# A decoder step with 32 routed experts on one core: slots of a tile numbered across groups of four partitions, and another order of work in the last three tiles

## The chip, the cores and the metric

The kernel runs on one core of a Trainium2 chip. The metric is the device time of one launch in microseconds (us), the median of several runs. A clock of 1 of TensorE (PE) is full speed; the profile calls VectorE DVE, ScalarE ACT, GpSimd POOL and the synchronisation engine SP. SP and POOL issue most of the transfers, and sixteen DMA engines carry them out.

## What is computed

One layer for 576 tokens (512 of a prompt and 64 of a sample) of 1024 channels, all in float32:

```python
m, new_pool, new_conv = _mixer(x, ...)            # w_in, pooling and short convolution, w_out
x = _layer_norm(DEEPNORM_ALPHA * x + m, ln1_g, ln1_b)
f = _hier_moe(x, ...)                             # top-1 of 4 groups, then top-2 of its 8 experts
x = _layer_norm(DEEPNORM_ALPHA * x + f, ln2_g, ln2_b)
...
for e in range(N_EXPERTS):                        # 32 experts, d_expert 512
    hdn = jax.nn.silu(xf @ w1[e]) * (xf @ w3[e])
    acc = acc + combine[:, e:e + 1] * (hdn @ w2[e])
```

Each token goes to two experts, so there are 1152 assignments. Every expert has three matrices of 2 MB (w1, w3, w2), 201 MB in all. By the reference's routing of the given inputs the experts get between 15 and 74 tokens, 36 on average.

## The kernel before, in words

**Front part** (to about 230 us). The mixer, the first layer norm, the router and a small index computation on DVE. DVE counts tokens and gives every assignment a tile and a slot in it.

**Tiles.** A tile is up to 64 tokens of one expert. There are 33 tiles, numbered 0 to 32 (E is 32): one per expert, and a second one for the expert with 74. `hot_first` and `hot_col` are one-hot comparisons of an assignment's slot number with a row of 64 numbers, `iota`, which holds 0 to 63. So slot s of a tile stands at position s of 64, the tokens of an expert fill positions 0, 1, 2 and so on, and the rest of the 64 are empty. From these tables come `token_row`, `pair_row`, `first_row`, `final_row` and `sample_row`, the lists of row numbers for GpSimd's indirect transfers. An empty position has a row number out of range, and nothing is moved for it.

**A tile on PE** (`tile(t)`, `into_hidden` L701, `turn_hidden` L714, `down` L722): w1 product (L710, 32 matmuls into bank B1), w3 product (L710, 32 matmuls), transposition of the hidden rows (L719), w2 product (L731, 16 matmuls of 512 columns). Two tiles share one fetch of x and one transposition of it (`turn_pair`, L698). Up to tile 30 (`STAGGERED`) the w2 product of tile t-1 is done within tile t. From tile 30 on each tile does its own too, so the program of PE ends: w1(30), w3(30), w2(29), w2(30), w1(31), w3(31), w2(31), w1(32), w3(32), w2(32). Positions 0 to 63 of SBUF hold channels 0 to 511 of the result of a tile, and 64 to 127 hold channels 512 to 1023 of the same 64 tokens.

**The other engines.** ACT: `silu_of(t)` (L950) after the w1 product, `spread(t)` (L992, a square root) for the second layer norm, `keep_xeT`, `fill` (the residual). DVE: `products(t)` (L1493) multiplies silu, gate and w3 product and frees PE to transpose; `keep_hT(t)` (L1498) copies the transposed hidden rows, for which w2(t) waits; `add_y(t)` (L1504) takes the result out of PSUM; `final(t)` (L1510 to L1529, 13 instructions) is the second layer norm of the tokens whose second expert is tile t. In `final`, L1528 waits for ACT's `spread(t)`.

**GpSimd's transfers** (2 KB per token and half, 4 KB per token for the fetch): `fetch` (L1107) gathers x for two tiles, `store(t)` (L1085) scatters the results of tokens for which t is the first of their two experts into `first_outputs`, `load(t)` (L1089) gathers those of the tokens for which t is the second, `send(t)` (L1093, L1097) scatters finished rows to the two outputs. `load(t)` waits for `store(t-1)` to have landed.

**Weights.** SP issues the loads of the 99 matrices in the order of use (`LOADS`) into ten blocks of 2 MB in SBUF; a block is loaded again once PE has used it. Each of these loads lies over all 128 partitions and is spread over the 16 DMA engines. PE waits for a block until all 16 have finished their part. The last w2 is loaded in two halves with a semaphore each (`last_half`).

Of the kernel before, what the change touches and what calls it, by code (L numbers as in the profile page):

```python
# [7 lines left out]
BF16 = mybir.dt.bfloat16  # L8
I32 = mybir.dt.int32
ALU = mybir.AluOpType  # L10
# [3 lines left out]
P = 128  # L14
D = 1024
KD = D // P
# [87 lines left out]
def build(nc, x_prompt, x_sample, state_pool, state_conv, w_in, w_pool_map, pool_scale, conv_w, w_out,  # L104
# [3 lines left out]
    with ctx:  # L108
        def sem(name):
            return ctx.enter_context(nc.semaphore(name))  # L110
# [66 lines left out]
        ones = sb("ones", [P, P], BF16)  # L177
        iota = sb("iota", [P, SLOTS])
        rev = sb("rev", [P, EPG])
        edges = sb("edges", [P, NQ])  # L180
        tokval = sb("tokval", [P, NT])
        row_shift = sb("row_shift", [P, 1])
        half_of = sb("half_of", [P, 1])
        chan = sb("chan", [P, NG, 4])
# [150 lines left out]
        more_first = sem("more_first")  # L335
        last_loaded = sem("last_loaded")
        prev_cleared = sem("prev_cleared")
        prev_loaded = [sem(f"prev_loaded{w}") for w in range(ZR)]
# [27 lines left out]
        def _(sp):  # L366
# [64 lines left out]
            def load(n):  # L431
                kind, t = LOADS[n]
                if kind == "w2" and t == E:
# [63 lines left out]
        def _(pe):  # L497
# [202 lines left out]

            def into_hidden(kind, b, loads, seq, i):  # L701

                done, bank = (h1_done, B1) if kind == "w1" else (h_done, B3)
                w = in_block(b)
                wait(pe, silu_ready if kind == "w1" else h_ready, seq)
                pe.wait_ge(block_loaded[b], loads)
                for k in range(KD):
                    x = xeT[:, k, i * SLOTS:(i + 1) * SLOTS]
                    for g in range(2):
                        mm = pe.matmul(ps[64 * g:64 * g + 64, bank, 0:FH], x, w[:, k, g * FH:(g + 1) * FH],  # L710
                                       start=(k == 0), stop=(k == KD - 1))
                mm.then_inc(done, 1)
# [38 lines left out]
            def tile(t):  # L751

                if t % 2 == 0:
                    pe.wait_ge(xeT_ready, t + 2)
                into_hidden("w1", *place("w1", t), t, t % 2)
                if t <= STAGGERED:
                    turn_hidden(t - 1)
                into_hidden("w3", *place("w3", t), t, t % 2)
                if t % 2:
                    turn_pair((t + 1) // 2)  # L760
                if t <= STAGGERED:
                    down(*place("w2", t - 1), t - 1)

            def last_half():
                pe.wait_ge(last_loaded, 16)

            def extra_tile(v):
# [39 lines left out]
        def _(act):  # L807
# [202 lines left out]
            fill(1, 1)  # L1010
            for t in range(2, E):
                if t == E - 1:
                    spread(t - 2)
                silu_of(t)
                if t % 2:
                    keep_xeT((t + 1) // 2)
                    fill((t + 1) // 2, 0)
                if 2 < t < E - 1:
                    spread(t - 2)
                if t % 2 and t < E - 1:  # L1020
                    fill((t + 1) // 2, 1)
            spread(E - 2)
            spread(E - 1)
            silu_of(E)
            spread(E)
# [14 lines left out]
        def _(pool):  # L1040
# [15 lines left out]
            g.memset(logits[:, NT - 1, :], 0.0)  # L1056
            g.iota(iota[:, :], [[1, SLOTS]], base=0, channel_multiplier=0, allow_small_or_imprecise_dtypes=True)
            g.iota(rev[:, :], [[-1, EPG]], base=EPG, channel_multiplier=0, allow_small_or_imprecise_dtypes=True)
            g.iota(edges[:, :], [[SLOTS, NQ]], base=SLOTS, channel_multiplier=0, allow_small_or_imprecise_dtypes=True)
# [81 lines left out]
            for t in range(2, E):  # L1141
                load(t - 1)
                store(t - 1)
                if t % 2 == 0 and t // 2 + 2 <= PAIRS:
                    fetch(t // 2 + 2)
                if t > 2:
                    send(t - 2)
# [38 lines left out]
        def _(dve):  # L1186
# [161 lines left out]
            dve.wait_ge(consts_made, 2)  # L1348
            settled(v.tensor_scalar(half_of[:, :], tokval[:, 0:1], float(SLOTS + 1), None, ALU.is_ge))
            v.tensor_scalar(row_shift[:, :], half_of[:, :], -2.0, None, ALU.add)  # L1350
            for j in range(4):
# [57 lines left out]
            for i in range(2):  # L1409
                v.tensor_tensor(hot_first[:, i, :, :], iota[:, :].unsqueeze(1).to_broadcast([P, NT, SLOTS]),  # L1410
                                slot_of[:, i, :].unsqueeze(2).to_broadcast([P, NT, SLOTS]), ALU.is_equal).then_inc(hot_ready, 1)
# [49 lines left out]

            v.tensor_tensor(hot_col, row(iota[:, :], A), col.unsqueeze(2).to_broadcast([P, A, SLOTS]), ALU.is_equal)
            settled(v.tensor_tensor(hot_tile, row(iota[:, 0:TILES], A),
# [43 lines left out]

            def finish(t, u, w, in_order):
# [3 lines left out]
                norm2(t, w, in_order)  # L1512

            def norm2(t, w, in_order):

# [9 lines left out]
                dve.sem_inc(var_ready, 1)  # L1525
                v.scalar_tensor_tensor(prev[w], prev[w], gap[:, 1:2], ln2[:, 0, :], ALU.subtract, ALU.mult)
                dve.wait_ge(std_ready, t + NT)
                in_order(v.reciprocal(gap[:, 0:1], std[:, :]))  # L1528
                v.scalar_tensor_tensor(prev[w], prev[w], gap[:, 0:1], ln2[:, 1, :], ALU.mult, ALU.add).then_inc(final_ready, 1)  # L1529

            def final(t):
# [4 lines left out]
                finish(t, t % YR, w, settled)  # L1536

# [43 lines left out]
            for t in range(2, STAGGERED + 1):  # L1581
                keep_hT(t - 1)
                products(t)
                add_y((t - 1) % YR, t - 1)
                if t > 2:
                    final(t - 2)
            keep_hT(E - 2)
            add_y((E - 2) % YR, E - 2)
# [4 lines left out]
            final(E - 2)  # L1593
            final(E - 1)
            products(E)
            keep_hT(E)
# [41 lines left out]
```

## Time and profile before

| | |
|---|---|
| median of 3 runs | 718.89 us (716.98 to 719.15) |
| the profiled execution's own time | 721.73 us |
| its span | 720.0 us |
| PE busy | 606.8 us, 84% |
| DVE, ACT, POOL busy | 306.4, 217.8, 160.5 us |
| bytes moved | 235.99 MB |

The span runs from the first to the last instruction. The profiled execution took 1.7 us more than its span, and 2.84 us more than the median of the three runs. A view of windows gives for a stretch the busy time of each engine, the granted clock of PE (PEclk) and the mean busy share of the 16 DMA engines (DMA share).

### The profile page before, as it was taken

How to read it: one execution, taken by the hardware profiler on the slowest of the kernel's cores; microseconds unless marked ns; L12 is line 12 of the kernel's file. 1: busy time of each engine (PE TensorE's matmuls, PEld its weight loads, DVE VectorE, ACT ScalarE, POOL GpSimd, SP SyncE). 2: the span in 40 equal slices, each digit the busy share in tenths (PEclk: the TensorE clock that was granted, in tenths of full speed). 3: DMA queues.
4: the chain of work that ended last, by engine and by line, in shares of the span. 5: the costliest groups of instructions: out<-in, count | busy, mean ns of one | idle time of the engine just before them, and what ended most of it. 6: DMA issues, size and time to landing. Idle time of an engine off the chain costs nothing.

```text
span 720.0 us, 10587 instructions
## 1 busy us (share of the span) xinstructions
PE 606.8 (84%) x4200; PEld 413.8 (57%) x4200; DVE 306.4 (43%) x786; ACT 217.8 (30%) x315; POOL 160.5 (22%) x182
## 2 busy tenths in 40 slices
PE   6999999999989999999977787677777768786772
PEld 5999999878845555555544444343444435443440
DVE  3562485426685033545443333333343333333452
ACT  3333313202210234345324241432324241432130
POOL 1000000000002124434332223222322323222341
PEclk9999999999999999999999999999999999999895
DMA  9863033833588999999999999999999999999930
GB/s 254 235 223 114 20 118 117 352 145 148 202 338 330 328 417 417 417 415 417 421 414 417 420 422 418 421 421 418 421 422 417 419 419 423 420 417 417 396 154 7
DMA packets 45754, 235.99 MB, mean 328 GB/s; under 512 B 13683, under 2 KB 18291, under 8 KB 28728
## 3 DMA queue, kind: packets, MB, share of 16 engines
q1 hardware_dynamic: 32303, 220.92, 76.3%
q0 software_dynamic: 12544, 11.71, 4.9%
q10 hardware_dynamic: 857, 2.67, 0.9%
q8 instruction: 34, 0.56, 0.3%
q14 instruction: 16, 0.13, 0.0%
HBM read 237.69 MB, written 30.20 MB: 372 GB/s over the span
## 4 chain that ended last, share of the span: by engine, by line
PE 44%; SPq 37%; DMA 7%; issue 4%; DVE 4%; POOL 1%; ACT 1%; POOLq 0%; DVEq 0%; ACTq 0%
SPq L404 26%; PE ps L547 14%; PE ps L710 12%; SPq L408 10%; PE ps L604 7%; PE ps L731 7%; DMA blocks<-in_w 6%; DMA blocks<-in_w_in 1%; SPq L428 1%; PE ps L633 1%; PE ps L679 1%; PE ps L698 1%; PE ps L617 1%; PE ps L719 1%; DVE blocks L1243 1%
## 5 line engine op out<-in xcount | busy, mean ns | idle before, releaser
L710 PE MATMUL ps<-blocks,ln 128*64 128x256 f32 x1888 | 217.3, 383 | 44.4 <-DMA blocks<-in_w 42.6
L710 PEld LDWEIGHTS ps<-blocks,ln 128*64 128x64 f32 x1888 | 148.5, 138 | 115.0 <-issue 65.0
L731 PE MATMUL ps<-blocks,hT 128*64 128x512 f32 x496 | 121.8, 635 | 35.2 <-DMA blocks<-in_w 27.4
L731 PEld LDWEIGHTS ps<-blocks,hT 128*64 128x64 f32 x496 | 35.8, 145 | 102.8 <-issue 67.0
L992 ACT ACTIVATE std<-rstd,eps 128x1 f32<-128x1 f32 x32 | 9.4, 294 | 234.3 <-DVEq L1525 129.8
L1493 DVE SCALAR_TENSOR_TENSOR h_rows<-silu,slot_gate,ps 128x256 f32<-128x256 f32 x33 | 15.8, 480 | 113.6 <-PE ps L710 103.4
L1089 POOL DMA_INDIRECT prev<-first_outputs,final_row x32 | 33.9, 1060 | 81.6 <-DMA first_outputs<-ye,first_row 47.0
L1093 POOL DMA_INDIRECT out<-prev,final_row x32 | 32.1, 1002 | 89.2 <-DVE prev L1529 88.9
L1504 DVE TENSOR_TENSOR ye_more<-ye_more,ps 128x512 f32<-128x512 f32 x16 | 11.0, 688 | 78.3 <-PE ps L731 78.3
L809 ACT ACTIVATE ln<-ps 128x512 f32<-128x512 f32 (+1 forms) x38 | 20.0, 572 | 78.0 <-PE ps L698 43.2
L547 PE MATMUL ps<-xT_high,w_in_high 128*128 128x288 f32 x256 | 40.5, 300 | 3.2 <-ACT w_in_high L809 2.0
L950 ACT ACT_TABLE_LOAD x30 | 38.5, 1283 | 11.9 <-PE ps L710 11.3
L1504 DVE TENSOR_TENSOR ye<-ye,ps 128x512 f32<-128x512 f32 x16 | 11.0, 688 | 72.7 <-PE ps L731 72.7
L547 PE MATMUL ps<-xT_low,w_in_high 128*128 128x288 f32 x256 | 40.0, 299 | 0.0
L547 PE MATMUL ps<-xT_high,w_in_low 128*128 128x288 f32 x256 | 39.7, 298 | 0.0
L992 ACT ACT_TABLE_LOAD x30 | 38.5, 1283 | 0.5
L547 PEld LDWEIGHTS ps<-xT_high,w_in_high 128*128 128x128 f32 x256 | 35.8, 188 | 4.1 <-ACT w_in_high L809 2.3
L547 PEld LDWEIGHTS ps<-xT_low,w_in_high 128*128 128x128 f32 x256 | 36.5, 192 | 0.0
L547 PEld LDWEIGHTS ps<-xT_high,w_in_low 128*128 128x128 f32 x256 | 36.4, 191 | 0.0
L1085 POOL DMA_INDIRECT first_outputs<-ye,first_row x16 | 18.4, 1151 | 78.3 <-DVE ye L1504 77.4
L1097 POOL DMA_INDIRECT out<-prev,sample_row x32 | 31.5, 984 | 9.9 <-issue 9.9
L1211 DVE TENSOR_TENSOR w_in_low<-blocks,w_in_high 128x1024 fp32r<-128x1024 f32 x16 | 19.6, 1224 | 32.2 <-ACT w_in_high L809 32.2
(234 smaller groups left out, 773.8 us busy)
## 6 DMA issues: line engine op xcount, KB each, us to landing
blocks<-in_w SPq DMA_DIRECT2D x86, 2048.0 KB
tenth_block<-in_w SPq DMA_DIRECT2D x9, 2048.0 KB
blocks<-in_w_in SPq DMA_DIRECT2D x3, 2048.0 KB, 12.0
blocks<-in_w_out SPq DMA_DIRECT2D x2, 2048.0 KB, 7.8
x_tok<-in_x_prompt SPq DMA_DIRECT2D x4, 512.0 KB, 5.4
blocks<-in_w_in SPq DMA_DIRECT2D x4, 512.0 KB, 11.5
first_outputs<-in_x_prompt SPq DMA_DIRECT2D x4, 512.0 KB, 8.7
x_rows<-x_tok ACTq DMA_DIRECT2D x4, 512.0 KB, 2.8
```

The source lines that it names most:

```text
L404: sp.dma_start(in_block(b), src.rearrange("(p c) f -> p c f", c=KD)).then_inc(block_loaded[b], 16)
L408: sp.dma_start(out_block(b).rearrange("p (g c) d -> p g c d", g=2), src.rearrange("(g p c) d -> p g c d", g=2, c=KF // 2)).then_inc(block_ ...
L547: mm = pe.matmul(ps[:, 2 * (c % 2) + h, 0:HALF], w_part[a][:, c % 2, k, :], xT[b][:, k, h * HALF:(h + 1) * HALF], start=(i == 0 and k == 0 ...
L604: mm = pe.matmul(ps[0:r, o % 4, :], mix_part[a][:, k, j * P:j * P + r], wout_part[h][b][:, k, :], start=(i == 0 and k == 0), stop=(i == 2 ...
L710: mm = pe.matmul(ps[64 * g:64 * g + 64, bank, 0:FH], x, w[:, k, g * FH:(g + 1) * FH], start=(k == 0), stop=(k == KD - 1))
L731: mm = pe.matmul(ps[64 * g:64 * g + 64, BY, :], hT[:, k % 2, k // 2 * SLOTS:(k // 2 + 1) * SLOTS], w[:, k, g * DH:(g + 1) * DH], start=(k ...
L950: nc.scalar.activation(silu, ps[:, B1, 0:FH], ACT.Silu).then_inc(silu_ready, 1)
L992: nc.scalar.activation(std[:, :], rstd[:, 1, 1:2], ACT.Sqrt, bias=eps[:, 1:2]).then_inc(std_ready, 1)
L1089: return g.indirect_dma_start(out=prev[w], out_offset=None, in_=first_rows[:, :], in_offset=rows_at(idx), bounds_check=last_row, oob_is_er ...
L1093: return g.indirect_dma_start(out=prompt_rows[:, :], out_offset=rows_at(idx), in_=prev[w], in_offset=None, bounds_check=last_prompt_row, o ...
L1097: return g.indirect_dma_start(out=sample_rows[:, :], out_offset=rows_at(idx), in_=prev[w], in_offset=None, bounds_check=last_sample_row, o ...
L1504: v.tensor_tensor(ye[u], ye[u], ps[:, BY, :], ALU.add).then_inc(y_kept, 1)
```

## The change

1. A second row of numbers, `slots`, takes the place of `iota` in the two one-hot comparisons. The 64 positions are seen as 2 halves of 32, each of 8 groups of four neighbours. Slots 0 to 15 go to the first two places of the eight groups of the first half (0 to 7 upwards, 8 to 15 back), 16 to 31 to the other two places, 32 to 63 in the same way into the second half. The row begins 0, 15, 16, 31, 1, 14, 17, 30.
2. DVE: `keep_hT(30)` stands before `final(28)` and not after it; `products(32)` stands inside `final(31)`, after its L1526, and not after it.
3. ACT: `silu_of(31)` before `spread(29)`, `silu_of(32)` before `spread(31)`.
4. GpSimd: `store(30)` before `load(30)`.
5. The w3 matrix of tile 32 is loaded in two halves (`last_in_loaded`), and PE waits for the second half after the 16th of the 32 matmuls.
6. One instruction on DVE (`half_of`, L1349) is folded into the next.

```diff
+            into = slots[:, :].rearrange("p (h e q o) -> p h e q o", h=2, e=8, q=2)
+            g.iota(into[:, :, :, :, 0], [[32, 2], [1, 8], [16, 2]], base=0, channel_multiplier=0,
+                   allow_small_or_imprecise_dtypes=True)
+            g.iota(into[:, :, :, :, 1], [[32, 2], [-1, 8], [16, 2]], base=15, channel_multiplier=0,
+                   allow_small_or_imprecise_dtypes=True)
...
-                v.tensor_tensor(hot_first[:, i, :, :], iota[:, :].unsqueeze(1).to_broadcast([P, NT, SLOTS]),
+                v.tensor_tensor(hot_first[:, i, :, :], slots[:, :].unsqueeze(1).to_broadcast([P, NT, SLOTS]),
...
-            v.tensor_tensor(hot_col, row(iota[:, :], A), col.unsqueeze(2).to_broadcast([P, A, SLOTS]), ALU.is_equal)
+            v.tensor_tensor(hot_col, row(slots[:, :], A), col.unsqueeze(2).to_broadcast([P, A, SLOTS]), ALU.is_equal)
...
+                if kind == "w3" and t == E:
...
+                    for g, landed in ((0, block_loaded[HOME[n]]), (1, last_in_loaded)):
+                        sp.dma_start(in_block(HOME[n])[:, g * KH:(g + 1) * KH, :],
+                                     src[:, g * KH:(g + 1) * KH, :]).then_inc(landed, 16)
...
+                    if halfway and k == KH:
+                        halfway()
...
             for t in range(2, E):
+                silu_of(t)
                 if t == E - 1:
                     spread(t - 2)
-                silu_of(t)
...
             spread(E - 2)
+            silu_of(E)
             spread(E - 1)
-            silu_of(E)
             spread(E)
...
             for t in range(2, E):
-                load(t - 1)
+                if t < E - 1:
+                    load(t - 1)
                 store(t - 1)
+                if t == E - 1:
+                    load(t - 1)
...
                 v.scalar_tensor_tensor(prev[w], prev[w], gap[:, 1:2], ln2[:, 0, :], ALU.subtract, ALU.mult)
+                if between:
+                    between()
                 dve.wait_ge(std_ready, t + NT)
...
                 add_y((t - 1) % YR, t - 1)
+                if t == STAGGERED:
+                    keep_hT(t)
                 if t > 2:
                     final(t - 2)
-            keep_hT(E - 2)
             add_y((E - 2) % YR, E - 2)
...
             final(E - 2)
-            final(E - 1)
-            products(E)
+            final(E - 1, lambda: products(E))
             keep_hT(E)
             last_final()
```

Where the instructions stand on DVE in tile 30, before. The rows are `keep_hT(29)`, `products(30)`, `add_y(29)` and the begin of `final(28)`:

```order
L1498 COPY hT<-ps 128x256
L1493 SCALAR_TENSOR_TENSOR h_rows<-silu,slot_gate,ps 128x256
L1504 TENSOR_TENSOR ye<-ye,ps 128x512
L1510 TENSOR_TENSOR prev<-prev,ye 128x512
L1516 BN_STATS stats<-prev 128x6
```

The same place in the change:

```order
L1517 COPY hT<-ps 128x256
L1512 SCALAR_TENSOR_TENSOR h_rows<-silu,slot_gate,ps 128x256
L1523 TENSOR_TENSOR ye<-ye,ps 128x512
L1517 COPY hT<-ps 128x256
L1529 TENSOR_TENSOR prev<-prev,ye 128x512
L1535 BN_STATS stats<-prev 128x6
```

The second copy of hT is `keep_hT(30)`; before, it stood behind the twelve further rows of `final(28)`.

The end of DVE's program before: the end of `final(31)`, then `products(32)`, `keep_hT(32)` and the begin of `last_final`:

```order
L1526 SCALAR_TENSOR_TENSOR prev<-prev,rstd,ln_68 128x512
L1528 RECIPROCAL rstd<-std 128x1
L1529 SCALAR_TENSOR_TENSOR prev<-prev,rstd,ln_68 128x512
L1493 SCALAR_TENSOR_TENSOR h_rows<-silu,slot_gate,ps 128x256
L1498 COPY hT<-ps 128x256
```

And in the change:

```order
L1545 SCALAR_TENSOR_TENSOR prev<-prev,rstd,ln_68 128x512
L1512 SCALAR_TENSOR_TENSOR h_rows<-silu,slot_gate,ps 128x256
L1549 RECIPROCAL rstd<-std 128x1
L1550 SCALAR_TENSOR_TENSOR prev<-prev,rstd,ln_68 128x512
L1517 COPY hT<-ps 128x256
```

`products(32)` has moved two instructions up, ahead of the wait for ACT's square root.

ACT's end before, with its waits: `spread(30)` and `spread(31)`, `silu_of(32)`, `spread(32)`:

```order
L992 ACTIVATE std<-rstd,eps 128x1 [waits var_ready] x2
L950 ACT_TABLE_LOAD [waits h1_done]
L950 ACTIVATE silu<-ps 128x256 [waits h_ready]
L992 ACT_TABLE_LOAD
L992 ACTIVATE std<-rstd,eps 128x1 [waits var_ready]
```

And in the change:

```order
L1004 ACTIVATE std<-rstd,eps 128x1 [waits var_ready]
L962 ACT_TABLE_LOAD [waits h1_done]
L962 ACTIVATE silu<-ps 128x256 [waits h_ready]
L1004 ACT_TABLE_LOAD
L1004 ACTIVATE std<-rstd,eps 128x1 [waits var_ready] x2
```

The silu of the last tile no longer stands behind `spread(31)`.

## Rows read from the trace of the kernel before

**Rows 1.** The page, the span in 40 slices of 18 us: DMA busy, in tenths.

```profile
DMA  9863033833588999999999999999999999999930
```

**Rows 2.** The page, DMA queues: GpSimd's own queue (packets, MB, share of 16 engines).

```profile
q0 software_dynamic: 12544, 11.71, 4.9%
```

**Rows 3.** Who waited for whom: us in total, times, longest.

```profile
PE ps L710 <- DMA blocks<-in_w: 42.6, 32, 2.5
...
PE ps L731 <- DMA blocks<-in_w: 27.4, 17, 2.6
```

**Rows 4.** Windows: length, busy by engine, then PEclk, DMA share, GB/s.

```profile
560.00:660.00 100.00, 75.57 (x536) 45.20 (x532) 33.89 (x97) 31.13 (x43) 29.50 (x28) 0.98 1.01 419
...
672.00:696.00 24.00, 23.08 (x166) 14.05 (x162) 11.94 (x35) 5.94 (x9) 7.86 (x9) 0.93 0.70 290
```

**Rows 5.** Windows at the end of the weight stream, same columns.

```profile
672.00:676.00 4.00, 4.00 (x12) 1.22 (x10) 0.00 (x0) 0.00 (x0) 1.11 (x2) 0.58 0.98 407
...
695.00:696.00 1.00, 0.68 (x7) 0.18 (x3) 0.92 (x4) 0.00 (x0) 0.70 (x2) 1.00 0.06 25
...
697.00:698.00 1.00, 0.00 (x0) 0.00 (x0) 0.96 (x3) 0.98 (x2) 0.84 (x1) 1.00 0.10 25
```

**Rows 6.** Timeline, tile 30: start, us, instruction, idle before it and its releaser.

```profile
650.30 3.67 PE L710 MATMUL ps<-blocks,ln 128*64 128x256 f32 x32 [1.60 <-DMA blocks<-in_w]
...
655.28 3.67 PE L710 MATMUL ps<-blocks,ln 128*64 128x256 f32 x32 [0.88 <-DMA blocks<-in_w]
...
660.53 3.65 PE L731 MATMUL ps<-blocks,hT 128*64 128x512 f32 x16 [1.57 <-DMA blocks<-in_w]
...
664.31 0.69 DVE L1504 TENSOR_TENSOR ye<-ye,ps 128x512 f32<-128x512 f32 x1 [4.76 <-PE ps L731]
...
669.42 0.42 DVE L1498 COPY hT<-ps 128x256 f32<-128x256 f32 x1
...
669.99 6.29 PE L731 MATMUL ps<-blocks,hT 128*64 128x512 f32 x16 [5.37 <-DVE hT L1498]
```

**Rows 7.** Timeline, tiles 31 and 32 on PE and DVE.

```profile
679.55 3.63 PE L710 MATMUL ps<-tenth_block,ln 128*64 128x256 f32 x32
...
685.12 3.65 PE L731 MATMUL ps<-blocks,hT 128*64 128x512 f32 x16 [0.61 <-DVE hT L1498]
...
688.89 0.69 DVE L1504 TENSOR_TENSOR ye_more<-ye_more,ps 128x512 f32<-128x512 f32 x1 [3.91 <-PE ps L731]
...
697.00 0.75 DVE L1526 SCALAR_TENSOR_TENSOR prev<-prev,rstd,ln 128x512 f32<-128x512 f32 x1 [0.16 <-DVE rstd L1524]
...
698.95 0.48 DVE L1493 SCALAR_TENSOR_TENSOR h_rows<-silu,slot_gate,ps 128x256 f32<-128x256 f32 x1 [0.35 <-ACT silu L950]
...
699.49 0.70 PE L719 MATMUL ps<-ident,h_rows 128*128 128x128 f32 x2 [3.81 <-DVE h_rows L1493]
...
700.80 6.25 PE L731 MATMUL ps<-blocks,hT 128*64 128x512 f32 x16 [0.61 <-DVE hT L1498]
```

**Rows 8.** Timeline of POOL: store(30), load(31), load(32), and the last send.

```profile
677.36 1.20 POOL L1085 DMA_INDIRECT first_outputs<-ye_more,first_row  x1 [2.59 <-DVE ye_more L1504]
...
685.91 1.05 POOL L1089 DMA_INDIRECT prev<-first_outputs,final_row  x1 [1.75 <-DMA first_outputs<-ye_more,first_row]
...
697.15 1.51 POOL L1089 DMA_INDIRECT prev<-first_outputs,final_row  x1 [0.30 <-issue]
...
713.21 0.98 POOL L1097 DMA_INDIRECT out<-prev,sample_row  x1 [0.30 <-issue]
```

**Rows 9.** Timeline: the instruction on DVE that goes, and a row of numbers made by POOL.

```profile
154.78 0.14 DVE L1349 TENSOR_SCALAR half_of<-tokval 128x1 f32<-128x1 f32 x1
...
2.37 0.18 POOL L1057 IOTA iota<- 128x64 f32 x1
```

More of the change, by code:

```diff
@@ L178, in build @@
         iota = sb("iota", [P, SLOTS])
+        slots = sb("slots", [P, SLOTS], BF16)
         rev = sb("rev", [P, EPG])
@@ L182, in build @@
         row_shift = sb("row_shift", [P, 1])
-        half_of = sb("half_of", [P, 1])
         chan = sb("chan", [P, NG, 4])
@@ L336, in build @@
         last_loaded = sem("last_loaded")
+        last_in_loaded = sem("last_in_loaded")
         prev_cleared = sem("prev_cleared")
@@ L432, in load @@
                 kind, t = LOADS[n]
-                if kind == "w2" and t == E:
+                if kind == "w3" and t == E:
+                    e = expert_of(t)
+                    src = w3[bass.DynSlice(e, 1)].rearrange("e d f -> (e d) f").rearrange("(p c) f -> p c f", c=KD)
+                    for g, landed in ((0, block_loaded[HOME[n]]), (1, last_in_loaded)):
+                        sp.dma_start(in_block(HOME[n])[:, g * KH:(g + 1) * KH, :],
+                                     src[:, g * KH:(g + 1) * KH, :]).then_inc(landed, 16)
+                elif kind == "w2" and t == E:
                     e = expert_of(t)
@@ L699, in turn_pair, with into_hidden @@
                     mm.then_inc(xe_turned, 1)
-            def into_hidden(kind, b, loads, seq, i):
+            def into_hidden(kind, b, loads, seq, i, halfway=None):
                 done, bank = (h1_done, B1) if kind == "w1" else (h_done, B3)
@@ L757, in tile @@
                     turn_hidden(t - 1)
-                into_hidden("w3", *place("w3", t), t, t % 2)
+                into_hidden("w3", *place("w3", t), t, t % 2, last_in_half if t == E else None)
                 if t % 2:
@@ L765, in last_half, with last_in_half @@
                 pe.wait_ge(last_loaded, 16)
+            def last_in_half():
+                pe.wait_ge(last_in_loaded, 16)
             def extra_tile(v):
@@ L1348, in _ @@
             dve.wait_ge(consts_made, 2)
-            settled(v.tensor_scalar(half_of[:, :], tokval[:, 0:1], float(SLOTS + 1), None, ALU.is_ge))
-            v.tensor_scalar(row_shift[:, :], half_of[:, :], -2.0, None, ALU.add)
+            v.tensor_scalar(row_shift[:, :], tokval[:, 0:1], float(SLOTS + 1), -2.0, ALU.is_ge, ALU.add)
             for j in range(4):
@@ L1506, in _, with finish @@
             own, other, both_of, gap = mv[:, :], rstd[:, 0, :], rstd[:, 1, :], rstd[:, 2, :]
-            def finish(t, u, w, in_order):
+            def finish(t, u, w, in_order, between=None):
                 dve.wait_ge(y_kept, t + 1)
@@ L1511, in finish, with norm2 @@
                 dve.sem_inc(prev_added, 1)
-                norm2(t, w, in_order)
-            def norm2(t, w, in_order):
+                norm2(t, w, in_order, between)
+            def norm2(t, w, in_order, between=None):
                 in_order(v.bn_stats(stats[:, 0, :], prev[w]))
@@ L1529, in norm2, with final @@
                 v.scalar_tensor_tensor(prev[w], prev[w], gap[:, 0:1], ln2[:, 1, :], ALU.mult, ALU.add).then_inc(final_ready, 1)
-            def final(t):
+            def final(t, between=None):
                 w = (t - 1) % ZR
@@ L1535, in final @@
                     dve.wait_ge(ln2_loaded, 64)
-                finish(t, t % YR, w, settled)
+                finish(t, t % YR, w, settled, between)
             def last_final():
```

## The prediction

> **What bounds the kernel now.** I read the slices first: from about 230 us to the last two slices the DMA engines are nearly full [rows 1]. The windows say it in numbers: in the 100 us before 660 the sixteen engines are busy all the time (share 1.01, 419 GB/s) while PE computes for 75.6 us [rows 4]. The waits give the direction: PE waited 42.6 and 27.4 us for weight blocks [rows 3]. So the tile part runs at the pace of the weight stream. Up to tile 30 each product starts when its block lands: w1(30) at 650.30, w3(30) at 655.28, w2(29) at 660.53 [rows 6].
>
> The stream's end is uneven. If all sixteen engines had the same work, the share would fall from 1 to 0 at once. It is 0.98 in 672 to 676 and 0.06 in 695 to 696, which is one engine of sixteen, and between 672 and 696 it is 0.70 on average [rows 4, 5]. The first engine runs dry some 22 us before the last. A block counts as landed when its slowest part is there, so PE has followed the slowest engine.
>
> Behind that, the last three tiles lose time on their own. w2(30) waits 5.37 us for the copy of hT, which stands on DVE behind a whole `final`, and then runs in 6.29 us where the same 16 matmuls took 3.65; the granted clock was 0.58 in 672 to 676, so part of this ran at the lower of PE's two levels [rows 5, 6]. The last w2 comes after another wait of 3.81 us, with DVE in `final(30)` and `final(31)` and ACT's silu behind `spread(31)`, and takes 6.25 us [rows 7]. It ends at 707.05. From there to the span's end at 720.0 are 12.95 us: the last `final`, the last send [rows 8] and its landing.
>
> **Part 1, the slots.** The empty positions of a tile cost nothing, so what counts is which engine serves the filled ones. [...] GpSimd's queue took 4.9% of 720 us on 16 engines [rows 2], 35.3 us each, for 5684 rows: 0.099 us per row, small packets included. [...]
>
> How much earlier would a level stream end? Blocks follow each other by 5.1 us in [rows 6], or by 5.3 us if 2.1 MB go at 419 GB/s [rows 4] less the 5% of GpSimd's queue; I take 5.2. Seven blocks after 660.5 the last one has landed: 696.9. By the windows the engines idled (1.01 - 0.70) x 24 = 7.4 us on average up to 696, and 15 of 16 of them the last 0.9 us: 8.3 us. That is the upper end. The heaviest engine keeps 24 rows over the mean, 2.3 us. **The stream ends 6.0 us earlier**, at 690.9; the lower end is 0.
>
> The two extra rows of numbers on POOL are some 0.2 us each at the very start [rows 9], while everybody waits for x. The instruction taken from DVE is 0.14 us at 154.8 [rows 9], in a stretch that I credit with nothing; it is no more than 0.14.
>
> **Parts 2 to 5, the last three tiles, with the stream 6.0 us earlier.** The blocks land at 659.7 (w2(30)), 664.9, 670.1, 675.3 (w2(31)), 680.5, 683.1 and 685.7 (the halves of w3(32)), 688.3 and 690.9 (those of w2(32)).
> - Tile 30: w2(29) runs 654.5 to 658.2. `add_y(29)` (0.69) and the copy of hT (0.42) now come first on DVE, so hT is there at 659.4, and w2(30) starts with its block at 659.7. The wait of 5.37 us goes, and with it, I take it, the lower clock. `final(28)` stands behind the copy, 0.4 us later; nobody waits for it in time.
> - Tile 31: w3(31) runs 670.1 to 673.8. From its end to w2(31) it took 685.12 - 683.18 = 1.9 us [rows 7], so w2(31) starts at 675.7, 0.4 us after its block, and ends at 679.4. ACT's silu now precedes `spread(29)`. This can hold `final(29)` for a silu and a change of tables, while DVE has to be free only at 673.8; I cost it at nothing.
> - DVE then runs `add_y(31)`, `final(30)` and `final(31)` up to L1526: 697.75 - 688.89 = 8.9 us [rows 7]. From 679.5 this gives 688.4. w3(32) ends 1.8 us after its second half has landed at 685.7 (or after w1(32), 680.5 + 3.7, and its own 3.7): 687.9. So `products(32)` runs 688.4 to 688.9. Here the halves gain nothing; without them w3(32) would end at 689.4 and cost 1.0 us.
> - From `products` to w2(32) it took 700.80 - 699.43 = 1.4 us [rows 7]. The two instructions of `final(31)` that now stand in between take 0.95 us and fit beside PE's transposition but for 0.15. w2(32) starts at 690.4 and runs, after waits of 2 us at most, at full clock: 3.65 us, end at 694.1. The second half, at 690.9, is in time for matmul 9 at 692.2.
> - GpSimd: `load(32)` waits for `store(31)` to land. A store took 685.91 - 678.56 = 7.35 us to land in the loaded queues [rows 8]. From 680.5 + 1.2 that gives 689.0, with the load's 1.5 us [rows 8] 690.6, and DVE wants the rows at 693.4. If landing takes nothing the cost is 0; if it takes a store's 7.35 us it is 4.5. Most of the stream is over by then, so it is nearer the lower end: 0.6. That `store(30)` precedes `load(30)` removes an obstacle for this chain; without it the store would wait for the landing of `store(29)`.
>
> The sum: PE ends at 694.1 where it ended at 707.05, -12.95; +0.6; **-12.4 us**. 6.0 of it is the stream, the rest the waits and the lower clock at the end. The span of 720.0 becomes 707.6, that execution's 721.73 becomes 709.3, and the median, 2.84 us below it, becomes **706.5**. The best of all bounds (8.3 and no late load) gives 703.6.
>
> **The rivals.**
> - **The levelling doesn't come** (0.12): the rows are dealt otherwise than I assume. All times above move by 6.0 and the order of the last tiles alone gains 6.4: 712.5. For it: no view names the engine that serves a row. Against: the size of the unevenness.
> - **The two lightest engines are light for a reason** (0.08). [...]
> - **The end is held by something else** (0.15): `load(32)` lands late, or w2(32) runs at the lower clock once more (6.25 for 3.65 us). 2.6 to 4.5 us come back: 709 to 711.
> - **Slower**: the new numbers put distant tokens on neighbouring partitions, and what was an ascending list of rows is so no longer. If a row costs more for that, the 35.3 us of GpSimd's queue grow on every engine, and the stream with them. The point at which it decides is a factor of 1.35 (12.4 / 35.3); with 1.5 the kernel would take 17.6 - 12.4 = 5 us more: 724. Against it: the tokens of one expert are on average 16 rows of x apart already (576 tokens, 36 to a tile), so there is little order to lose. 0.04.
> - **Nothing measurable** happens, the gain being lost somewhere: 0.02.
>
> **How the numbers follow.** My forecast has 0.59. The range goes from 702.5 (the best of the bounds, 703.6, less 1.1 us for the scatter of the three runs) to 713.0, which takes in the first three rivals. About 0.3% (2 us) is what a measurement of this kernel can tell from no change. Faster by more: 0.59 + 0.12 + 0.08 + 0.15 = 0.94; within: 0.02; slower: 0.04.
>
> **What would show it.** The DMA share stays at 1 until about 5 us before the stream's end and then falls within few us: slots right. A slow fall over 20 us: wrong. PE's wait for hT before w2(30) is gone and its 16 matmuls take 3.65 us. `products(32)` starts at L1526's end, near 688.4. w2(32) takes 3.65 us. A wait of DVE for the load of tile 32 would be the third rival, more busy time of q0 than 4.9% the fourth.

## The result, and the profile after

The changed kernel takes 708.43 us (median of 4 runs, 707.12 to 709.22), the kernel before 719.02 us (716.98 to 720.08). The measured ratio is 0.9832, with a 95% interval from 0.9807 to 0.9858; the two medians by themselves give 0.9853, that is 10.6 us less. Two repetitions on other occasions gave 0.9814 (0.9782 to 0.9846) and 0.9826 (0.9802 to 0.985). The forecast was 706.5 us within 702.5 to 713.0, and faster by more than 0.3% with a chance of 0.94.

The profiled execution took 707.71 us, its span is 706.0. The page of the kernel after, DMA busy in tenths of 40 slices, and GpSimd's queue, which answer to [rows 1, 2]:

```profile
DMA  9953033834497999999999999999999999999990
...
q0 software_dynamic: 12544, 11.71, 4.9%
```

The slices are full (9 of 10) up to the last but one, and GpSimd's queue has the same packets, bytes and share. The 5684 filled rows of 2 KB are 11.64 of its 11.71 MB, so no rows are moved for the empty positions; that these cost no time either was not shown. Who waited for whom in the kernel after:

```profile
PE ps L719 <- DMA blocks<-in_w: 45.0, 34, 2.6
...
PE ps L740 <- DMA blocks<-in_w: 24.8, 20, 2.2
```

PE still waits for weight blocks [rows 3]: the stream sets the pace as before, it is only shorter. Its end, in windows of the kernel after (length, busy by engine, PEclk, DMA share, GB/s):

```profile
676.00:680.00 4.00, 2.15 (x12) 0.54 (x10) 1.65 (x3) 0.00 (x0) 0.82 (x1) 1.00 0.99 399
680.00:684.00 4.00, 4.00 (x38) 3.23 (x40) 3.62 (x13) 0.60 (x2) 0.68 (x2) 1.00 1.02 415
684.00:688.00 4.00, 3.34 (x32) 2.29 (x27) 3.37 (x14) 2.94 (x4) 2.96 (x3) 1.00 0.70 283
688.00:690.00 2.00, 1.22 (x8) 0.54 (x9) 0.86 (x2) 0.00 (x0) 1.00 (x1) 1.00 0.34 108
...
691.00:692.00 1.00, 0.73 (x4) 0.34 (x6) 0.38 (x1) 0.00 (x0) 0.11 (x1) 1.00 0.08 15
```

Before, the share fell from 672 on over some 22 us [rows 4, 5]. Now it is full to 684 and gone at 691: seven us. That is what sixteen engines that finish closer together would give.

The last tiles in the timeline of the kernel after, in the order of [rows 6, 7]:

```profile
653.40 3.65 PE L740 MATMUL ps<-blocks,hT 128*64 128x512 f32 x16 [1.39 <-DMA blocks<-in_w]
...
657.17 0.69 DVE L1523 TENSOR_TENSOR ye<-ye,ps 128x512 f32<-128x512 f32 x1 [4.57 <-PE ps L740]
657.78 0.42 DVE L1517 COPY hT<-ps 128x256 f32<-128x256 f32 x1
...
658.70 3.65 PE L740 MATMUL ps<-blocks,hT 128*64 128x512 f32 x16 [1.22 <-DMA blocks<-in_w]
...
670.84 0.16 DVE L1549 RECIPROCAL rstd<-std 128x1 f32<-128x1 f32 x1 [3.65 <-ACT std L1004]
...
674.44 3.65 PE L740 MATMUL ps<-blocks,hT 128*64 128x512 f32 x16 [0.61 <-DMA blocks<-in_w]
...
687.19 0.48 DVE L1512 SCALAR_TENSOR_TENSOR h_rows<-silu,slot_gate,ps 128x256 f32<-128x256 f32 x1
...
689.01 1.94 PE L740 MATMUL ps<-blocks,hT 128*64 128x512 f32 x8 [0.79 <-DVE hT L1517]
...
691.27 1.94 PE L740 MATMUL ps<-blocks,hT 128*64 128x512 f32 x8 [0.33 <-DMA blocks<-in_w]
...
691.62 0.69 DVE L1564 TENSOR_TENSOR prev<-prev,ye 128x512 f32<-128x512 f32 x1 [2.76 <-DMA prev<-first_outputs,final_row]
```

hT is copied at 657.78, and w2(30) waits for its block, not for DVE. The w2 products of tiles 29 to 32 run at full clock (1.00 in 653 to 657, 658 to 663, 674 to 678 and 689 to 693.3): 3.65 us each, the last one in two pieces of 1.94 us with a wait for the second half of its matrix between them. In the kernel before, w2(30) and w2(32) had a granted clock of 0.57 and 0.58 on average; its windows of 2 us from 700 to 706 give 0.50, the lower level, where 650 to 660 gives 1.00. DVE waits 2.76 us for `load(32)`, but its result is added only when w2(32) ends at 693.21, so this costs nothing.

**Where the time went.** Each profile can be cut at the first w2 product (w2(0), with which the front part ends) and at the start of w2(29), which comes after a wait for its block in every kernel here. The first w2 of the kernel before and of the kernel after:

```profile
227.60 1.94 PE L731 MATMUL ps<-blocks,hT 128*64 128x512 f32 x8 [0.43 <-DVE hT L1498]
```

```profile
226.18 1.94 PE L740 MATMUL ps<-blocks,hT 128*64 128x512 f32 x8 [0.43 <-DVE hT L1517]
```

| us | front | stream, up to w2(29) | from there to the end | span |
|---|---|---|---|---|
| before | 227.6 | 432.9 | 59.5 | 720.0 |
| after | 226.2 | 427.2 | 52.6 | 706.0 |
| difference | -1.4 | -5.7 | -6.9 | -14.0 |

The front differs by up to 2.5 us among all the kernels of this study (225.2 to 227.7), whatever the numbering, and among three profiles of the changed kernel by 1.0 (225.5 to 226.5), so I ascribe its 1.4 us to scatter. The cut is not one between the two parts of the change: seven blocks of the stream still land in the last stretch. Without the front the difference of the profiles is 12.6 us, and the three ratios give 12.1, 13.4 and 12.5 us (the differences of the medians 10.6, 13.9 and 11.9).

### The profile page after: what moved, and what is told of

Read it like the earlier page. It is cut to its first block, busy times and chain, and to the rows that moved or that the text cites. A ratio compares the mean times of both kernels' runs of the same rounds, so it can differ in the third digit from the quotient of the medians.

```text
span 706.0 us, 10591 instructions
## 1 busy us (share of the span) xinstructions
PE 600.4 (85%) x4200; PEld 413.1 (59%) x4200; DVE 306.9 (43%) x785; ACT 217.7 (31%) x315; POOL 160.9 (23%) x184
## 3 DMA queue, kind: packets, MB, share of 16 engines
q0 software_dynamic: 12544, 11.71, 4.9%
## 4 chain that ended last, share of the span: by engine, by line
PE 43%; SPq 39%; DMA 6%; DVE 6%; issue 3%; ACT 1%; POOL 0%; POOLq 0%; DVEq 0%; ACTq 0%
SPq L405 27%; PE ps L554 14%; SPq L409 12%; PE ps L719 11%; PE ps L611 7%; DMA blocks<-in_w 6%; PE ps L740 6%; SPq L429 1%; PE ps L640 1%; PE ps L632 1%; PE ps L517 1%; PE ps L705 1%; PE ps L624 1%; PE ps L728 1%; DMA x_tok<-in_x_prompt 1%
## 5 line engine op out<-in xcount | busy, mean ns | idle before, releaser
L740 PE MATMUL ps<-blocks,hT 128*64 128x512 f32 x496 | 113.4, 597 | 26.0 <-DMA blocks<-in_w 24.8
L740 PEld LDWEIGHTS ps<-blocks,hT 128*64 128x64 f32 x496 | 33.6, 136 | 87.0 <-issue 53.9
L1102 POOL DMA_INDIRECT first_outputs<-ye_more,first_row x16 | 18.9, 1181 | 67.6 <-DVE ye_more L1523 66.4
L719 PE MATMUL ps<-tenth_block,ln 128*64 128x256 f32 x224 | 27.4, 399 | 7.6 <-DMA tenth_block<-in_w 7.6
```

Source lines behind the costliest of these rows:

```text
L740: mm = pe.matmul(ps[64 * g:64 * g + 64, BY, :], hT[:, k % 2, k // 2 * SLOTS:(k // 2 + 1) * SLOTS], w[:, k, g * DH:(g + 1) * DH], start=(k ...
L1102: return g.indirect_dma_start(out=first_rows[:, :], out_offset=rows_at(idx), in_=ye[u], in_offset=None, bounds_check=last_row, oob_is_err= ...
```

## The experiments

The first four of the table ran beside one another (the kernel before 720.13 us, 22 runs), the next four too (720.94, 9 runs), and the last four (720.59, 11 runs). The last four columns are those of the table above.

| kernel | median | ratio and interval | front | stream | last tiles | span |
|---|---|---|---|---|---|---|
| slots_only | 713.92 | 0.9913 (0.9885 to 0.994) | 226.0 | 426.9 | 57.7 | 710.6 |
| order_only | 713.78 | 0.9904 (0.9874 to 0.9934) | 225.8 | 432.0 | 54.2 | 712.0 |
| piled_groups | 724.54 | 1.0066 (1.0043 to 1.009) | 226.4 | 443.0 | 52.8 | 722.2 |
| plain_turns | 708.27 | 0.985 (0.9794 to 0.9905) | 226.2 | 427.0 | 53.9 | 707.1 |
| whole_again | 707.07 | 0.9814 (0.9782 to 0.9846) | 225.5 | 426.8 | 52.4 | 704.7 |
| reversed_groups | 708.37 | 0.9821 (0.9791 to 0.9851) | 227.7 | 427.2 | 53.8 | 708.7 |
| hT_late | 714.96 | 0.9904 (0.987 to 0.9939) | 227.1 | 427.0 | 59.3 | 713.4 |
| products_late | 710.08 | 0.9859 (0.9822 to 0.9896) | 225.6 | 427.3 | 54.6 | 707.5 |
| whole_third | 708.65 | 0.9826 (0.9802 to 0.985) | 226.5 | 427.0 | 52.5 | 706.0 |
| whole_w3 | 710.89 | 0.9865 (0.9838 to 0.9893) | 225.4 | 426.9 | 53.8 | 706.1 |
| acts_and_stores_old | 710.1 | 0.9842 (0.9818 to 0.9867) | 225.2 | 427.2 | 52.5 | 704.9 |
| slots_and_hT | 714.01 | 0.9916 (0.9886 to 0.9946) | 225.2 | 427.5 | 57.3 | 710.0 |

A stretch of a single profile is free of the front's scatter, so I read effects of 1 to 2 us from the stretches and the larger ones from both. Two profiles of different executions can still differ by chance in the last tiles. In whole_again, whole_w3, acts_and_stores_old and slots_and_hT the profiled execution was the fastest of its kernel, in reversed_groups the slowest.

### The numbers alone, and the order alone

slots_only takes the parts 2 to 5 of the change back:

```diff
-                if kind == "w3" and t == E:
...
+            spread(E - 1)
             silu_of(E)
-            spread(E - 1)
...
-                if t == E - 1:
-                    load(t - 1)
...
-                if t == STAGGERED:
-                    keep_hT(t)
...
+            keep_hT(E - 2)
...
-            final(E - 1, lambda: products(E))
+            final(E - 1)
+            products(E)
```

> The new numbers alone, the order of the last three tiles as in the kernel before. Theory L (the row of numbers levels the work of the DMA engines, and the weight stream ends some 6 us earlier): 6.0 us less than the kernel before, 713.0 us; the wait of w2(30) for hT and the lower clock behind it are there as before. Rival O (all of the gain is from the order of the last tiles): no change, 719.

Measured: 6.2 us less than before, and the stream of 426.9 us has the whole change's length. The last tiles have their old waits (5.37 us for hT again), and yet take 1.8 us less than before: w2(30) ran in 4.97 us (granted clock 0.73) and w2(32) in 5.21 (0.69), where before it was 6.29 and 6.25. So some of what the last stretch gained comes with the numbers, or by chance, and not from the order.

order_only keeps the parts 2 to 5 and compares with the old row:

```diff
-                v.tensor_tensor(hot_first[:, i, :, :], slots[:, :].unsqueeze(1).to_broadcast([P, NT, SLOTS]),
+                v.tensor_tensor(hot_first[:, i, :, :], iota[:, :].unsqueeze(1).to_broadcast([P, NT, SLOTS]),
...
-            v.tensor_tensor(hot_col, row(slots[:, :], A), col.unsqueeze(2).to_broadcast([P, A, SLOTS]), ALU.is_equal)
+            v.tensor_tensor(hot_col, row(iota[:, :], A), col.unsqueeze(2).to_broadcast([P, A, SLOTS]), ALU.is_equal)
```

> The order of the last three tiles and the halves of the last w3 alone, slots numbered as before. Theory L: 6.4 us less than before, 712.5 us, with the DMA share falling over 22 us as before. Rival O: 708.5, as the whole change. If the parts hide one another, the two single changes add up to more or to less than the whole change's 10.6 us.

Measured: 6.4 us less than before; the stream is nearly as long as before (432.0 against 432.9), and its end falls slowly as before. Windows of order_only:

```profile
668.00:672.00 4.00, 3.67 (x32) 2.63 (x32) 3.15 (x11) 0.00 (x0) 3.08 (x4) 1.00 0.98 411
...
688.00:690.00 2.00, 2.00 (x20) 1.25 (x18) 1.74 (x6) 1.97 (x3) 1.49 (x2) 1.00 0.51 209
...
692.00:693.00 1.00, 0.51 (x2) 0.32 (x2) 0.96 (x3) 0.00 (x0) 0.51 (x1) 1.00 0.20 66
```

Its last tiles took 54.2 us with w2(32) at 5.35 us (granted clock 0.68). Rival O falls with both runs. The two changes add up within the scatter: by the medians 6.2 + 6.4 = 12.6 us, where the whole gave 10.6, 13.9 and 11.9.

### How rows are dealt to the engines

piled_groups fills the first and the ninth group before the second and the tenth. If these two share an engine, as its expectation supposes, the filled positions pile up on few engines:

```diff
-            into = slots[:, :].rearrange("p (h e q o) -> p h e q o", h=2, e=8, q=2)
-            g.iota(into[:, :, :, :, 0], [[32, 2], [1, 8], [16, 2]], base=0, channel_multiplier=0,
-                   allow_small_or_imprecise_dtypes=True)
-            g.iota(into[:, :, :, :, 1], [[32, 2], [-1, 8], [16, 2]], base=15, channel_multiplier=0,
+            into = slots[:, :].rearrange("p (h e c) -> p h e c", h=2, e=8)
+            g.iota(into, [[4, 2], [8, 8], [1, 4]], base=0, channel_multiplier=0,
```

> The change with slots numbered so that the filled positions pile up on few engines if rows are dealt out by groups of four with the ninth group again on the first engine: slots 0 to 7 on groups 1 and 9, 8 to 15 on groups 2 and 10, and so on. Counted rows for the heaviest engine 636 against 379 in the change and 476 before. Theory L: 257 rows more than in the change at 0.08 to 0.10 us, 20 to 26 us slower than the change: 729 to 734 us. If eight neighbours went to one engine: heaviest 646 against 574 in the change, 6 to 7 us slower. If rows were dealt out one by one: 468 in both, no difference.

Measured: 724.54 us, 16 us above the change and slower than the kernel before (1.0066). The stream of 443.0 us is 16 us longer than with the new numbers and 10 us longer than with the old. Windows of piled_groups:

```profile
600.00:620.00 20.00, 15.75 (x120) 9.97 (x121) 6.07 (x17) 3.72 (x7) 7.32 (x7) 1.00 1.01 419
...
640.00:660.00 20.00, 15.04 (x107) 8.59 (x105) 7.75 (x20) 5.65 (x8) 6.47 (x6) 1.00 0.97 393
...
680.00:684.00 4.00, 3.58 (x32) 2.52 (x32) 2.73 (x10) 0.00 (x0) 3.09 (x4) 1.00 0.63 260
...
700.00:704.00 4.00, 3.45 (x30) 1.92 (x26) 3.18 (x12) 3.10 (x4) 3.35 (x3) 1.00 0.38 149
```

The share falls from about 20 us before the end and is still 0.38 when the last blocks land; already at 640 to 660 it is 0.97, as if some engines had run dry between blocks. Of the three ways of dealing that I counted, only the groups of four, repeated after 32 partitions, make this numbering so much worse: for eight neighbours I had expected 6 to 7 us, for single rows nothing. So for these gathers and scatters with empty rows the run speaks for groups of four with the ninth again on the engine of the first. How partitions 64 to 127 share the engines, which the counts need too, no run shows; there they are my estimate. They take the rows of 2 KB of all of GpSimd's transfers by the reference's routing, a row of x as two. The size was 16 us where 20 to 26 were expected. The expectation took the rows of all tiles, while the stretch ends at w2(29). Counted up to there (the fetches for tiles up to 31, all other transfers up to tile 27), the heaviest engine has 332 rows in the change, 420 in the kernel before and 551 with piled_groups: 88 and 219 more. That is 5.7 / 88 = 0.065 us and 16 / 219 = 0.073 us per row.

plain_turns fills the groups in plain turns:

```diff
+            into = slots[:, :].rearrange("p (h e c) -> p h e c", h=2, e=8)
+            g.iota(into, [[32, 2], [1, 8], [8, 4]], base=0, channel_multiplier=0,
```

> The change with the eight groups of a half filled in plain turns (slots 0, 8, 16, 24 on group 1, and 7, 15, 23, 31 on group 8), not there and back. Counted rows: 405 for the heaviest, which is an engine of the first group, and 327 and 309 for the two of the last group (379 and 363 in the change). Theory L with equal engines: 26 rows more, 2.1 to 2.6 us slower than the change: about 710.8. Rival S (the two engines of the last group are about 4 us slower than the others over the run): the change is held by one of them, and giving them fewer rows makes it up to 1.4 us faster: 707.

Measured: the stream has the same length as in the change (427.0), where 21 more rows on the heaviest engine up to w2(29) (26 in all) should cost 1.4 to 1.5 us at 0.065 to 0.073 each. So the count of the heaviest engine's rows gives the large differences, and missed this small one. The total of 708.27 us lies within the scatter of the change's three medians. So there and back is worth nothing that I can measure against plain turns; neither theory's number came out.

reversed_groups numbers the eight groups from the other end, so that the first and the last change places:

```diff
-            g.iota(into[:, :, :, :, 0], [[32, 2], [1, 8], [16, 2]], base=0, channel_multiplier=0,
+            g.iota(into[:, :, :, :, 0], [[32, 2], [-1, 8], [16, 2]], base=7, channel_multiplier=0,
...
-            g.iota(into[:, :, :, :, 1], [[32, 2], [-1, 8], [16, 2]], base=15, channel_multiplier=0,
+            g.iota(into[:, :, :, :, 1], [[32, 2], [1, 8], [16, 2]], base=8, channel_multiplier=0,
```

> The changed kernel with the eight groups of each half numbered from the other end (the row of numbers begins 7, 8, 23, 24 and ends 32, 47, 48, 63). By the count the same sixteen loads with the engines exchanged: the last group's engines get 353 and 335 rows in place of 379 and 363, the first group's 379 and 363. Equal engines (theory L): no difference from the whole change, within 1 us. Rival S (the last group's engines slower by 4 us): 2 us faster, and a smaller spread of the sixteen landings of a block than the 7 us in the change.

> The changed kernel once more, on the same chip as the next three. If the sum of the two single changes holds (6.2 and 6.3 us in the first four runs): 12 us less than the kernel before. If it is as in the first comparison: 10.6 less.

Measured: the stream is 427.2 us, with whole_again beside it at 426.8. The end falls alike too: in windows of 2 us from 30 us after the start of w2(29) on, the DMA share is 0.89, 0.72, 0.41, 0.20 and 0.05 in reversed_groups and 0.88, 0.74, 0.45, 0.20 and 0.06 in whole_again. Rival S had 2 us less and a smaller spread. It falls, and with it the prediction's second rival: by the count the two lightest engines of the kernel before are those of the last group. The span is longer than whole_again's by 4.0 us, 2.2 in the front, 0.4 in the stream and 1.3 in the last tiles, where this row of reversed_groups stands:

```profile
690.61 5.35 PE L740 MATMUL ps<-blocks,hT 128*64 128x512 f32 x16 [0.78 <-DVE hT L1517]
```

w2(32) fell to the lower clock within its 16 matmuls (granted clock 0.61 in 692 to 696) and took 1.7 us more than the usual 3.65; whole_again's waited 0.40 us between its two halves instead. plain_turns and order_only had the same 5.35 us; over these products the granted clock is 0.68 in all three.

### The parts of the new order, one by one

hT_late:

```diff
-                if t == STAGGERED:
-                    keep_hT(t)
                 if t > 2:
                     final(t - 2)
+            keep_hT(E - 2)
```

> The changed kernel with keep_hT(30) behind final(28) again. Theory T (the wait for hT pushes w2(30), w1(31), w3(31) and w2(31) back by 5 us, and the lower clock adds 2.6): w2(31) then ends some 4 to 5 us later, and with it the DVE chain that bounds the end: 4 to 5 us slower than the whole change. Rival (the blocks of tiles 31 and 32 land so late that PE catches up before the end): less than 1 us slower.

Measured: 7.9 us slower than whole_again by the medians, 6.9 us in the last tiles. PE in hT_late, with what it waited for:

```profile
663.59 6.33 PE L740 MATMUL ps<-blocks,hT 128*64 128x512 f32 x16 [5.37 <-DVE hT L1517]
...
679.28 3.65 PE L740 MATMUL ps<-blocks,hT 128*64 128x512 f32 x16 [0.61 <-DVE hT L1517]
...
693.10 0.70 PE L728 MATMUL ps<-ident,h_rows 128*128 128x128 f32 x2 [3.25 <-DVE h_rows L1512]
694.40 6.28 PE L740 MATMUL ps<-blocks,hT 128*64 128x512 f32 x16 [0.61 <-DVE hT L1517]
```

w2(30) waits and runs slowly (6.33 us at a granted clock of 0.57), and w2(31) ends 4.1 us late against w2(29)'s start, as expected. What I had missed is the last product: PE has caught up with the landed blocks, works w1(32) and w3(32) off without a pause, waits 3.25 us for DVE and runs w2(32) at the lower clock too (0.57 over its 6.28 us), 2.6 us more. The interval of the ratio (0.987 to 0.9939) lies clear of whole_again's.

products_late:

```diff
+            spread(E - 1)
             silu_of(E)
-            spread(E - 1)
...
-            final(E - 1, lambda: products(E))
+            final(E - 1)
+            products(E)
```

> The changed kernel with products(32) behind final(31) on DVE and silu(32) behind spread(31) on ACT again, as before. Theory T: silu(32) comes 1.7 us (table and silu) after spread(31), and w2(32) starts that much later; the second half of w2(32) had to wait for its block by 0.33 us, so that little of it is hidden: 1 to 2 us slower than the whole change, 4 if PE falls to its lower clock in the wait. Rival: within 0.5 us, hidden behind the stream's end.

Measured: 3.0 us slower by the medians, 2.2 in the last tiles. w2(32) starts only 1.0 us later (36.5 us after w2(29), 35.5 in whole_again), but runs in 5.35 us (granted clock 0.68). That this edit brings the lower clock is not shown: order_only, reversed_groups and plain_turns had it without the edit, with last tiles of 54.2, 53.8 and 53.9 us against 54.6 here. The intervals of the two ratios overlap, so what is shown for this part is the later start.

whole_w3:

```diff
-                if kind == "w3" and t == E:
...
-                    for g, landed in ((0, block_loaded[HOME[n]]), (1, last_in_loaded)):
...
-                into_hidden("w3", *place("w3", t), t, t % 2, last_in_half if t == E else None)
+                into_hidden("w3", *place("w3", t), t, t % 2)
```

> The changed kernel with the last w3 loaded in one piece again. Theory (the prediction's): w3(32) then starts when its whole block is there and ends 3.7 us later in place of 1.8 us after the second half, products(32) and w2(32) move by that, less what w2's second half waits for its own block anyway: 1 to 1.5 us slower than the whole change. Rival (the DVE chain or the stream's end hide it): within 0.5 us.

> The changed kernel a third time, beside the next three: 0.981 to 0.983 of the kernel before, 707 to 708.5 us.

Measured: 1.3 us more in the last tiles (53.8 against 52.5), the size that was expected; the medians lie 2.2 us apart, with intervals that overlap. The cause is not clean, though. PE and DVE in whole_w3:

```profile
683.88 3.67 PE L713 MATMUL ps<-blocks,ln 128*64 128x256 f32 x32 [1.67 <-DMA blocks<-in_w]
...
684.23 0.69 DVE L1523 TENSOR_TENSOR prev<-prev,ye_more 128x512 f32<-128x512 f32 x1 [1.92 <-DMA prev<-first_outputs,final_row]
...
687.89 0.47 DVE L1506 SCALAR_TENSOR_TENSOR h_rows<-silu,slot_gate,ps 128x256 f32<-128x256 f32 x1
...
689.71 3.65 PE L734 MATMUL ps<-blocks,hT 128*64 128x512 f32 x16 [0.78 <-DVE hT L1511]
```

w3(32) ends at 687.55, 1.7 us later after w2(29) than in whole_third. But `final(31)` also waited 1.92 us for the rows of `load(31)`, which it did not in whole_third, and `products(32)` followed it on DVE without an idle moment. I estimate from these rows that in this execution the halves alone would have brought nothing, and rows in time alone some 0.2 us: both held the end. The prediction's 1.0 us for the missing halves is neither confirmed nor refuted.

acts_and_stores_old:

```diff
-                silu_of(t)
                 if t == E - 1:
                     spread(t - 2)
+                silu_of(t)
...
-                if t < E - 1:
-                    load(t - 1)
+                load(t - 1)
                 store(t - 1)
-                if t == E - 1:
-                    load(t - 1)
```

> The changed kernel with silu(31) behind spread(29) and load(30) ahead of store(30), as in the kernel before; all else as changed. Theory (the prediction's): both cost nothing on the path, within 0.5 us of the whole change; store(30) goes out 2 to 3 us later, and load(31) with it, but final(31) takes its rows some 8 us after load(31). Rival: the later store(30) pushes load(31) and load(32) back until DVE waits for them, 1 to 2 us slower.

Measured: the last tiles take 52.5 us, the same. The medians differ by 1.5 us with intervals that overlap widely, and the profiled execution (706.62 us) is the fastest of six, the others 709.49 to 713.07. In its trace the old order costs nothing in the end: DVE waits 0.38 us for `load(31)` and w2(32) starts 0.6 us later than in whole_third (36.1 us after w2(29)), but finds both halves of its matrix landed and ends at the same distance, 39.8 us. That the two parts are worth nothing in every execution is not shown.

slots_and_hT has the new numbers and the earlier copy of hT, and nothing else of the change:

> The new numbers and the earlier keep_hT(30) alone, the other parts as in the kernel before. If the parts act as measured one by one (products and silu 3.0 us, the halves of w3 about 1 us or hidden behind the later silu): 3 to 4 us slower than the whole change, 710.5 to 712 us. If the other parts matter only together with each other: more than 4 us slower.

Measured: 5.4 us slower than whole_third by the medians, 4.8 in the last tiles, and only 0.4 us better there than slots_only. POOL and DVE in slots_and_hT:

```profile
667.08 1.13 POOL L1096 DMA_INDIRECT first_outputs<-ye_more,first_row  x1 [0.30 <-issue]
...
678.41 1.39 POOL L1100 DMA_INDIRECT prev<-first_outputs,final_row  x1 [7.61 <-DMA first_outputs<-ye_more,first_row]
...
685.26 0.69 DVE L1520 TENSOR_TENSOR prev<-prev,ye_more 128x512 f32<-128x512 f32 x1 [2.46 <-DMA prev<-first_outputs,final_row]
...
690.74 0.50 PE L722 MATMUL ps<-ident,h_rows 128*128 128x128 f32 x2 [2.86 <-DVE h_rows L1503]
...
691.86 5.35 PE L734 MATMUL ps<-blocks,hT 128*64 128x512 f32 x16 [0.61 <-DVE hT L1508]
```

With GpSimd's old order, `store(30)` goes out after `load(30)`, 14.3 us after w2(29) and not 12.3 as in the change. It had landed only at 678.41; `load(31)` starts then, and `final(31)` waits 2.46 us for its rows. silu(32) and `products(32)` stand behind that, and w2(32) starts 3.6 us later than in whole_third and runs in 5.35 us (granted clock 0.68). That the old order of GpSimd makes the rows late is not shown: acts_and_stores_old has the same order and waited 0.38 us (its `load(31)` went out at 676.17), while whole_w3 waited 1.92 us with the new one. But the parts are not worth a fixed sum each: taken back singly they cost 6.9, 2.2, 1.3 and 0.0 us in the last tiles, 10.4 together (14.6 by the medians), where all of them together are worth 57.7 - 52.5 = 5.2 us.

## Why the prediction was right

**The bound.** PE follows the slowest DMA engine: borne out. Of the 14 profiles the eleven with levelled numbers have a stream of 426.8 to 427.5 us, whatever the order of the last tiles, the two with the old numbers 432.0 and 432.9, and piled_groups 443.0. No view names the engine that serves a row, so the engines' part in it is inferred from these lengths and from the fall of the DMA share.

**The levelling, -6.0 us.** The stream was 5.7 us shorter in the first profile, 6.1 and 5.9 in the repetitions; measured against order_only, the other profile with the old numbers, it is 4.8 to 5.2. The price per row of the prediction, 0.099 us, was too high; the streams and the counted rows give 0.065 to 0.073. At that price the 279 rows that the count by groups of four puts between the most and the least loaded engine of the kernel before are 18 to 20 us; single rows (160) would give 10 to 12 and eight neighbours (586) 38 to 43, so the groups of four lie nearest to the 22 to 24 us over which its share fell. The 6.0 rested mainly on the idle share of the engines at the end, less 2.3 us for the rest of the unevenness (24 rows at 0.099 us are 2.4). That rest is larger than counted: the share falls over 7 us where the count's 45 rows between the extremes would be some 3 us. What keeps it up is open; it is not the last group's slowness. The 24 rows over the mean are from the count and no run shows them or their 2.3 us; the runs showed in their place a stream 5.7 to 6.1 us shorter, 2.2 to 2.6 us less than the upper end of 8.3.

**The last tiles, -6.4 us** with the late load. Their stretch gave 6.9, of which 1.8 had come in slots_only too; by order_only the order alone gave 5.3 in that stretch and 6.4 by the medians. Shifted by the front's 1.4 us, the points of the sum are, forecast and measured: w2(30) 659.7 and 660.1, w2(31) 675.7 and 675.9, `products(32)` 688.4 and 688.6, w2(32) 690.4 and 690.4, PE's end 694.1 and 694.6. From PE's end to the span's end it took 12.8 us, before 12.95. The 3.65 us that `final(29)` waited for ACT because of the earlier silu ended before `products(31)`, as costed.

**Terms that were off.** `load(32)` cost nothing (0.6 taken): its rows were there at 691.62 and their sum with ye was ready at 692.31, 1.0 us before DVE went on with w2(32)'s result at 693.33. The second half of w2(32) was to be in time for matmul 9; PE waited 0.33 us for it and started that matmul, shifted, at 692.7 where the forecast had 692.2. This is the 0.5 us at PE's end.

**The rivals.** No levelling: excluded by slots_only. A slow last group: excluded by reversed_groups; the 4 us of rival S were my estimate, 279 counted rows at 0.099 us, 27.7 us, less the 24 seen. Dearer rows: GpSimd's queue has its 4.9% as before. The third rival was not in the first profile, but it exists: in order_only, reversed_groups and plain_turns w2(32) took 5.35 us at a partly lower clock (0.68 on average), 1.7 us of the 2.6 that the rival gave.

**The last step, from the execution to the median.** The gain of 12.4 us was forecast for the profiled execution, 709.3 us; it took 707.71, 1.6 us less, of which the front's scatter is 1.4. For the median the prediction then took off 2.84 us, the distance of the one profiled execution of the kernel before from the median of three. That distance did not carry over: the profiled execution of the change lies 0.7 us below its median, and the kernel before had medians of 720.13 to 720.94 in 42 later runs, so that 718.89 was a low one. The two errors, 1.6 and 3.6 us, partly cancel, which is luck, and leave 708.43 against 706.5. The three medians of the changed kernel differ by 1.6 us by themselves.

## What to carry to other kernels

When all sixteen DMA engines carry one stream and a second, irregular traffic has empty rows, look at how the DMA share falls at the stream's end: a fall over 20 us, as here, can mean that the rows pile up on some engines, and another numbering tests it. Spread the filled positions over the groups of four partitions, which here made the stream 427.2 us where it was 432.9; plain turns did as well (427.0) as there and back. At the end of a program price the reordering of several engines as a whole: the earlier copy of hT alone left the last tiles only 0.4 us shorter than slots_only, because other waits stood behind the one removed.

## What the runs showed that I had not expected

- w2(32) ran at full clock (1.00 over the product) in all three profiles of the whole change and in whole_w3, and at a partly lower one (0.68) in reversed_groups, plain_turns and order_only (5.35 for 3.65 us), though PE came to it in nearly the same way: idle for 0.98 us before the transposition and 0.78 before the product in reversed_groups, 0.66 and 0.79 in the change. The length of these two idle stretches alone does not decide it: with 1.25 and 0.78 us in acts_and_stores_old the product ran at full clock (1.00). The scatter of the medians by 1 to 2 us may have this among its causes; that was not tested.
- A store by GpSimd takes long to land in full queues: in slots_and_hT the one issued at 667.08 for 1.13 us released its waiter at 678.41, 10.2 us later, with a DMA share of 1.02 in 668 to 677. In [rows 8] it was 7.35 us, with a share of 0.83 in 678 to 686.
- With 45 counted rows between the extremes, some 3 us at 0.065 to 0.073 us each, the DMA share still takes 7 us to fall.
